# One distance for each pair of weight buffers in a two-block fp32 kernel

## What is computed

```python
# first block: 256 tokens; D = 2048
z  = modulate(rms_norm(x), ...) @ w_in + b_in          # D x 13312
y  = sum over three branches of sigmoid(gate) * (branch @ w_branch)   # conv, sgu, attention: 1024 x D each
x  = x + mod * (y @ w_o + b_o)                         # D x D
x  = x + mod * (square(relu(h @ w1 + b1)) @ w2 + b2)   # D x 4D, 4D x D
# second block: 272 tokens
proj = rms_norm(h) @ attn_w_in                         # D x 4D
y  = (rms_norm(diff_attend(...)) * silu(g)) @ attn_w_out
u, g = split(rms_norm(h) @ pool_w_in)                  # D x 2D
y  = (grouped(mixed, w_group) * scale * silu(g)) @ pool_w_out
```

## Time and profile before

| | |
|---|---|
| median of 3 runs | 2742.77 us (2735.62 to 2748.8) |
| span of the profiled execution | 2741.3 us |
| its own time outside the span | not given |
| instructions | 51495 |
| busy | TensorE 98%, weight loads 94%, VectorE 70%, ScalarE 46%, GpSimd 6% |
| HBM | 533.57 MB read, 195 GB/s over the span |

### The profile page before, as it was taken

The page is one execution under the profiler, slowest core; times in us unless marked ns, Lnnn a source line. Parts: engine busy times, 40 slices in busy tenths (PEclk is TensorE's granted clock), DMA queues, the critical chain, the costliest instruction groups (busy, mean ns, idle before and its releaser), DMA issues.

```text
span 2741.3 us, 51495 instructions
## 1 busy us (share of the span) xinstructions
PE 2683.9 (98%) x21464; PEld 2565.5 (94%) x21464; DVE 1908.6 (70%) x2935; ACT 1268.4 (46%) x1836; POOL 153.2 (6%) x162
## 2 busy tenths in 40 slices
PE   7999999999999999999999999999999999999998
PEld 4599977899999999999999999999999999989997
DVE  6765689889898778886554555677656665478564
ACT  5522344455446445544443444464444444554453
POOL 0000001200014001100000000030000000100000
PEclk9999999999999999999999999999999999999999
DMA  8766765456556787787555555564444444535563
GB/s 305 289 219 223 236 187 175 139 201 186 198 185 195 253 281 270 257 275 240 185 186 198 179 191 187 187 197 154 160 133 149 156 148 148 175 120 190 185 195 130
DMA packets 163990, 539.01 MB, mean 197 GB/s; under 512 B 31024, under 2 KB 35120, under 8 KB 163632
## 3 DMA queue, kind: packets, MB, share of 16 engines
q1 hardware_dynamic: 163760, 535.73, 58.7%
HBM read 533.57 MB, written 2.10 MB: 195 GB/s over the span
## 4 chain that ended last, share of the span: by engine, by line
PE 88%; DVE 6%; DMA 3%; issue 2%; ACT 1%; SPq 0%; DVEq 0%; POOL 0%; ACTq 0%
PE ps L561 26%; PE ps L566 26%; PE ps L563 26%; DVE lo L1683 2%; DMA raw<-in_w_ff 2%; PE ps L777 1%; PE ps L796 1%; PE ps L724 1%; PE ps L712 1%; DMA raw<-in_w_mod 1%; PE ps L785 1%; DVE row L2259 1%; ACT hi L1071 1%; PE ps L674 1%; PE ps L952 0%
## 5 line engine op out<-in xcount | busy, mean ns | idle before, releaser
L1071 ACT ACTIVATE hi<-raw 128x1024 fp32r<-128x1024 f32 x856 | 901.3, 1058 | 908.4 <-PE ps L566 470.4
L561 PE MATMUL ps<-AH,hi 128*128 128x256 f32 (+2 forms) x4432 | 1264.2, 285 | 1.8 <-DVE AL L2098 1.8
L566 PE MATMUL ps<-AH,lo 128*128 128x256 f32 (+2 forms) x4432 | 1252.8, 283 | 7.4 <-DVE lo L1683 7.4
L563 PE MATMUL ps<-AL,hi 128*128 128x256 f32 (+2 forms) x4432 | 1254.1, 283 | 0.0
L1683 DVE TENSOR_TENSOR lo<-raw,hi 128x1024 fp32r<-128x1024 f32 x856 | 1039.9, 1228 | 204.5 <-ACT hi L1071 202.8
L561 PEld LDWEIGHTS ps<-AH,hi 128*128 128x128 f32 x4432 | 837.6, 189 | 31.1 <-issue 29.8
L566 PEld LDWEIGHTS ps<-AH,lo 128*128 128x128 f32 x4432 | 837.9, 189 | 10.4 <-DVE lo L1683 10.3
L563 PEld LDWEIGHTS ps<-AL,hi 128*128 128x128 f32 x4432 | 838.0, 189 | 0.9
L566 PE MATMUL ps<-YH,lo 128*128 128x256 f32 (+1 forms) x1512 | 422.1, 279 | 0.9 <-DVE lo L1683 0.8
L561 PE MATMUL ps<-YH,hi 128*128 128x256 f32 (+1 forms) x1512 | 422.0, 279 | 0.0
L563 PE MATMUL ps<-YL,hi 128*128 128x256 f32 (+1 forms) x1512 | 421.9, 279 | 0.0
(11 more groups left out here) (276 smaller groups left out, 2509.6 us busy)
## 6 DMA issues: line engine op xcount, KB each, us to landing
raw<-in_w_ff SPq DMA_DIRECT2D x256, 512.0 KB, 4.3
raw<-in_w_in SPq DMA_DIRECT2D x208, 512.0 KB, 4.1
raw<-in_w_mod SPq DMA_DIRECT2D x192, 512.0 KB, 5.0
raw<-in_w_ain SPq DMA_DIRECT2D x128, 512.0 KB, 3.8
raw<-in_w_pin SPq DMA_DIRECT2D x64, 512.0 KB, 3.5
raw<-in_w_o SPq DMA_DIRECT2D x32, 512.0 KB, 4.7
raw<-in_w_aout SPq DMA_DIRECT2D x32, 512.0 KB, 3.5
raw<-in_w_pout SPq DMA_DIRECT2D x32, 512.0 KB, 3.5
```

Of the source, the lines that this page charges most:

```text
L561: e.matmul(b.ap[:, o], hi[:, k, :], xh, start=start and k + i == 0, stop=False, skip_group_check=many)
L563: e.matmul(b.ap[:, o], hi[:, k, :], xl, start=False, stop=False, skip_group_check=many)
L566: mm = e.matmul(b.ap[:, o], los[j % NSPLIT][:, k, :], xh, start=False, stop=stop and k == KU - 1, skip_group_check=many)
L1071: e.activation(his[u % NSPLIT][:, :, :], raws[raw_at[i]][:, :].rearrange("p (k m) -> p k m", k=KU), ACT.Copy).then_inc(s_hi, 1)
```

## The change

Between the pairs of weight buffers come small unused tensors of 0, 32, 32, 64 and 64 bytes, and hi and lo of one number now stand side by side. So pair 0 stays 64 bytes behind the activations modulo 512, and pairs 1 to 4 are 96, 128, 192 and 256 bytes behind. A last unused tensor of 320 bytes brings everything that follows back to its old place modulo 512. The three tensors of ones become one, filled with 1/2048; where a mean is over 1024 or 256 values, ScalarE multiplies by 2 or 8 as it reads the sum (`scale` of an activation that is there already).

```diff
+STEPS = (0, 8, 8, 16, 16)
...
-        his = [sb(f"hi{i}", [128, KU, 128], F32R) for i in range(NSPLIT)]
-        los = [sb(f"lo{i}", [128, KU, 128], F32R) for i in range(NSPLIT)]
+        his, los = [], []
+        for i in range(NSPLIT):
+            if STEPS[i]:
+                sb(f"step{i}", [128, STEPS[i]])
+            his.append(sb(f"hi{i}", [128, KU, 128], F32R))
+            los.append(sb(f"lo{i}", [128, KU, 128], F32R))
+        sb("steps", [128, 128 - sum(STEPS)])
...
-        ones = {n: sb(f"ones{n}", [128, 128]) for n in (2048, 1024, 256)}
+        ones = sb("ones", [128, 128])
...
-            def mean(key, d, n, total=ssum, last=None):
+            def mean(key, n, total=ssum, last=None):
...
-                e.matmul(XB[:, 0:n], ones[d][:, :], sumv(total, n), start=True, stop=True).then_inc(s_mean, 1)
+                e.matmul(XB[:, 0:n], ones[:, :], sumv(total, n), start=True, stop=True).then_inc(s_mean, 1)
...
-            def root(row, n, free=None):
+            def root(row, n, free=None, count=2048):
...
-                e.activation(row[:, 0:n], XB[:, 0:n], ACT.Sqrt, bias=eps).then_inc(s_root, 1)
+                e.activation(row[:, 0:n], XB[:, 0:n], ACT.Sqrt, bias=eps,
+                             scale=2048.0 / count).then_inc(s_root, 1)
...
-                e.activation(mean[:, 0:T], XB[:, 0:T], ACT.Copy).then_inc(s_root, 1)
+                e.activation(mean[:, 0:T], XB[:, 0:T], ACT.Copy, scale=2.0).then_inc(s_root, 1)
...
-            for n, o in ones.items():
-                e.memset(o[:, :], 1.0 / n)
+            e.memset(ones[:, :], 1.0 / 2048)
```

More of the change, by code:

```diff
@@ L636, in turned_mean @@
                 for c, t in enumerate(CHUNKS[n]):
-                    e.matmul(XB[:, MCOL + c:MCOL + c + 1], ssum[:, t:t + 128], ones[2048][:, 0:1], start=(c == 0),
+                    e.matmul(XB[:, MCOL + c:MCOL + c + 1], ssum[:, t:t + 128], ones[:, 0:1], start=(c == 0),
                              stop=False, skip_group_check=True)
@@ L642, in turned_mean @@
                     mm = e.matmul(XB[:, MCOL + c:MCOL + c + 1], sqr[i % 2][:, max(t, 0):max(t, 0) + 128],
-                                  ones[2048][:, 0:1], start=False, stop=True, skip_group_check=True)
+                                  ones[:, 0:1], start=False, stop=True, skip_group_check=True)
                 mm.then_inc(s_mean, 1)
@@ L658, in _ @@
             e.wait_ge(s_setup, 1)
-            e.matmul(XB[:, 0:2], ones[2048][:, :], vt[:, LAMC:LAMC + 2], start=True, stop=True).then_inc(s_lamp, 1)
+            e.matmul(XB[:, 0:2], ones[:, :], vt[:, LAMC:LAMC + 2], start=True, stop=True).then_inc(s_lamp, 1)
             xb.free = (s_lame, 1)
@@ L673, in norms @@
                             e.wait_ge(s_sqx, 4 * c + k // 4 + 1)
-                        mm = e.matmul(XB[:, 0:T], ones[2048][:, :], squares[4 * c + k // 4][:, k % 4, :],
+                        mm = e.matmul(XB[:, 0:T], ones[:, :], squares[4 * c + k // 4][:, k % 4, :],
                                       start=(k == 0), stop=(k == 15))
@@ L822, in norm_means @@
                     yield
-                mean(first, 1024, T, last=ADD[first] + 8)
+                mean(first, T, last=ADD[first] + 8)
                 yield
@@ L826, in norm_means @@
                     yield
-                mean(second, 1024, T, last=ADD[second] + 8)
+                mean(second, T, last=ADD[second] + 8)
                 yield
@@ L901, in n2 @@
                 yield
-                mean("n2", 2048, T, last=ADD["n2"] + 16)
+                mean("n2", T, last=ADD["n2"] + 16)
             spawn(n2())
@@ L918, in last_norm @@
                     yield
-                mean("s1", 2048, T, last=ADD["s"] + 31)
+                mean("s1", T, last=ADD["s"] + 31)
                 e.wait_ge(s_m3, 1)
-                mean("s2", 2048, L, ssum2, ADD["s"] + 32)
+                mean("s2", L, ssum2, ADD["s"] + 32)
             spawn(last_norm())
@@ L979, in diff_head @@
                 yield
-                mean(f"on", 256, L, last=ADD["on"] + 2 * h + 2)
+                mean(f"on", L, last=ADD["on"] + 2 * h + 2)
                 xb.free = (s_root, MEAN["on"] + h + 1)
@@ L1020, in pin @@
                     yield
-                mean("pin", 2048, L, last=ADD["pin"] + 16)
+                mean("pin", L, last=ADD["pin"] + 16)
             spawn(pin())
@@ L1280, in layer_norm @@
                     yield
-                root(rows[ROW[second] % 2], T, (s_row, 2) if second == "sgv" else (s_xn, 8))
+                root(rows[ROW[second] % 2], T, (s_row, 2) if second == "sgv" else (s_xn, 8), 1024)
                 yield
@@ L1536, in diff_head @@
                 yield
-                root(rows[(ROW["on"] + h) % 2], L, (s_cn, 8) if h == 0 else (s_row, 3) if h == 1 else (s_oy, 2 * h - 2))
+                root(rows[(ROW["on"] + h) % 2], L, (s_cn, 8) if h == 0 else (s_row, 3) if h == 1 else (s_oy, 2 * h - 2),
+                     256)
                 yield
```

## The result

The changed kernel takes 2776.12 us (median of 4 runs, 2774.12 to 2777.69) against 2742.22 us for the kernel before (4 runs): a ratio of 1.0135, 95% interval 1.0121 to 1.015. It is 34 us slower, where 22 us were forecast.

A forecast was written before the change was run, and what follows sets the result against it. The prediction took TensorE's matmul spacing, how long one matmul holds back the next, as the bound. The profiled 2741.3 us plus 22 us for new distances in dense stages, other terms 0, gave 2763 us, range 2724 to 2785.

The forecast's parts named there:

- the noughts for the ones and scales: Single ones tensor: two fills fewer at the start, factors on existing activations; 0, or 0.3 us without cover.
- the middle between two prices: Dense matmuls at new distances: 2.35 ns more, between held 113.3 ns and walking 118.9 ns, giving +22 us.
- the likeliest case: Whole kernel: the forecast's own case, some +0.5% to +1.2%, 2755 to 2775 us, chance 0.41.
- term (a): Layout in dense stages: 9,370 of 11,712 matmuls get a new distance; bounds 8 us less and +44 us, taken +22 us.
- the walking stage: Slice of 256 columns out of the 288-wide layout, where the distance changes with k: 118.9 ns a matmul.
- rival 3: Dense stages: every new distance costs 118.9 ns like walking, or each switch sets the slow pace anew; 2785 us, chance 0.12.
- two walking sets: 288-wide stages: distances 64, 448, 320, 192 or 0, 384, 256, 128 as k advances, claimed equal to 0.6 ns.
- Rival 2: Stretch 840 to 1140: changing distances break up the slow pace, 10.5 us back; 2731 to 2718 us, chance 0.20.
- Rivals 1 and 4: Dense stages: any held distance is as good, or weight and activation streams never meet; 2741 us, together 0.27, the latter 0.03.
- term (b): 8,448 matmuls of the 288-wide stages: pairs keep or swap walking distances at equal price; 0, bound 2 us either way.

The follow-up runs named there:

- the side-by-side layout with all at 64: Kernel with all pairs at 64 and the hi and lo activations of one k side by side, against the kernel before: 2748.82 us, ratio 1.0032.

## Why the prediction was right, and where it was not

**The sign and the place.** That the loss would lie in the 11,712 dense matmuls, with counts, splits, waits and clock unchanged, held, but for the short stretch of clock named above. So did the noughts for the ones and scales (all at 64: +0.1%) and for ScalarE and VectorE (1058 and 1228 ns before and after). That the time fell inside the range and the sign was right is in part luck: the forecast took the middle between two prices, and any price for the new places above the mean of the kernel before gives a slower one. 2776 lies 1 us above what was called the likeliest case, 2755 to 2775.

**The size of term (a).** The step that was mis-sized is the middle price of 116.6 ns for the four new pairs. Measured they run at 119.0 on average, the very upper bound of 118.9 that I had taken from the walking stage, as rival 3 had it. 9,370 x (119.0 - 116.6) would be 22 us more than forecast, and 12.6 us more came. The kernel before stood at 114.7 and not at 114.2, since 20 units beside 840 to 1140 are slow too and the fast ones average 113.5: 5 us less. Pair 0 lost most of its slow units: 2342 x 0.65 = 2 us less.

The rest was made good elsewhere. Summed unit by unit, the 10,176 matmuls lose 33.4 us and the 1,536 of the first 300 us lose 5.3 us (114.4 to 117.8 ns), which the span shows in full: at 107.5 us the changed kernel is 0.4 us behind, at 314.1 us it is 5.6 us behind. The wide stages and the slice add 1.3 us. Of these 40 us, some 3 come back between 327 and 348 us, where the kernel before has the wait and the lower clock and the changed one has not, and some 2 between 1237 and 1262 us, where the waits of the kernel before for a lo half (0.8 us) and for `maccs` (0.6 us) are gone. Whether the distances or chance took these away the runs don't say; with all pairs at 64 the stretch of lower clock at 341 us is missing too.

**The reading behind it was wrong.** I read from two walking sets at one price that a distance which stays costs less than one which walks. All pairs at 256 never change distance and run at 119.9, and the wide stages with the walk taken out still run at 120.3 and 125.0. Nor do the two sets cost the same: the prediction read one at 256 columns and the other at 258 and 272. With all pairs at 256 the sets are exchanged, and the slice, with its 256 columns, walks the set that contains 64:

```profile
2585.00:2655.00 70.00, 70.00 (x602) 1.00 0.58 193
```

That is 70/600 = 116.7 ns, where the earlier trace rows gave 118.9 for the other set, while over all units 258 columns go from 120.3 to 120.8 and 272 from 125.2 to 125.9. So at one column count the two sets differ, by 2 ns in the slice, and what the wide stages pay beyond that was not taken away by any held distance. What the kernel before had was one special place, 64 modulo 256 at 256 columns, good to within 8 bytes, and the change left it for four pairs of five. The trace of before could not show that, as it never holds another distance; its rows bounded the price all but rightly (119.0 against 118.9), and nothing in them favoured the middle over the walking row.

**The rivals.** Rival 3, given 0.12, is what came about for the four new pairs: 117.9 to 120.1 ns where it said 118.9. Its 2785 us is 9 too many for the same reasons as above. Its other half, that each switch sets the slow pace anew, did not: pair 0 was slow in 9 of 85 units. Rival 2 was half seen: pair 0 did leave the slow pace (9 of 85 units), and ending it is worth what was said, but the four other pairs paid 9,370 x (119.0 - 114.7) = 40 us for 2. A kernel that ends it without leaving 64 gained 10 to 14 us. Rivals 1 and 4 are out: moving the weights by 192 bytes made the kernel 2.1% slower, of which 0.1% belongs to the rest of the change. The Trainium skill says in SBUF — State Buffer, section "SBUF: two separate sides", that TensorE never waits on anyone; the runs don't agree with what the prediction drew from it, that no placement could matter.

**The wide stages**, term (b), held to 0.4 ns at 258 and 272 columns; the slice moved by 0.7 ns, on 768 matmuls half a microsecond.

**What stays open.** The experiments price places; they don't show the mechanism, nor where in SBUF or TensorE the streams meet. The word distance is more than they prove: the hi activations start at byte 480 modulo 512 in every run, so a place of the weights by itself and a distance from the hi activations were never told apart. A run with all weights and all activations moved together would do it. The three overlaps are coupled, and the runs don't say through what; nor what starts the slow pace, and why the side-by-side layout with all at 64 fell into it for the whole feed-forward part, which may be its history or the higher bits of its addresses.

## What to carry to other kernels

Where TensorE is busy without a gap, divide a window's length by its count of matmuls: 2.6% of this kernel (2723 against 2794 us) lay in where its operands began in SBUF, and no wait or busy share shows it. Give several buffers different offsets in one run and read each one's units: fifteen places cost three runs, and the good one may be good only to within a few bytes. Don't vary what is at a good place, and compare paces only between matmuls of one column count. Price a combination as a whole: lo weights moved by 128 bytes gained 0.5%, and with the dense lo activations moved along the kernel lost 2%.

## What the runs showed of the hardware that was not expected

- The pace of a stream of fp32r matmuls with 256 columns goes by the start of the weights against the activations modulo 256 bytes (the hi activations never moved): 113.3 ns at best at 64 and at 320, unit means of 116.8 to 120.1 ns at the other multiples of 32, 117.8 already at 56 and 118.4 at 72.
- At 64 the stream has two paces, 113.3 and 117.7 ns, at a granted clock of 1.00 in both, and keeps one of them over up to 300 us (102 units in a row). With the lo weights at 192 no unit of 424 runs at the slow one, and a single such unit in five cuts the rows of slow units to four.
- With lo weights and lo activations both 128 bytes on, every overlap keeps its distance of 64, and the dense stream runs at 120.7 ns; with the lo activations left where they were, at 113.6.
- With 258 and 272 columns no pair of any run came below 119.5 and 124.3 ns in the mean, that is 12 and 11 ns over the columns' own time, against 6.6 at 256.
